# Seven column tiles of a projection as 2x2 block products with seven products (Strassen's form)

## The reference, cut to what matters

```python
xn = _rmsnorm(x, g_pre)          # x: 2048 prompt tokens and 8*8 sample tokens, 1024 wide
u = xn @ w_in                    # 1024 x IN_WIDTH, the part that the change touches
gq, gk, gv, gg, glr, dq, dk, dv, dg, ga, gb = jnp.split(u, cuts, axis=-1)
...
o_a, s_new = _gla(q, k, v, log_a, gla_s0)
...
o_g, lse_g = _dilated_prompt(qg, kg, vg, dil, span)      # g in three groups: (128,1), (512,4), (2048,16)
...
merged = jax.nn.sigmoid(ga) * y_a + jax.nn.sigmoid(gb) * y_b
h = x + _rmsnorm(merged @ w_out, g_post)
h = h + (pe @ w_ple_proj) * jax.nn.sigmoid(h @ w_ple_gate)
```

## Time and profile before

| | |
|---|---|
| time, median of 3 runs | 2802.56 us (2802.45 to 2804.43) |
| span of the profiled execution | 2799.7 us, 40580 instructions |
| time of the profiled execution itself | not recorded apart; its span is 2.9 us under the median |
| PE busy | 2769.4 us, 99% |
| DVE, ACT, POOL busy | 1077.3, 861.5, 360.3 us |
| column tiles 0 to 19 | about 0 to 2154 us |
| column tiles 9 to 15 | about 956 to 1723 us |
| the mix | about 2154 to 2800 us |

### The profile page before, as it was taken

One profiled execution on the slowest core, in us unless ns is written; L12 is line 12 of the kernel. 1 busy time (PEld: TensorE's weight loads), 2 busy tenths in 40 slices (PEclk: granted clock), 3 DMA queues, 4 the chain that ended last, 5 costly groups with the idle time before them and its releaser, 6 DMA issues.

```text
span 2799.7 us, 40580 instructions
## 1 busy us (share of the span) xinstructions
PE 2769.4 (99%) x16108; PEld 1453.6 (52%) x16108; DVE 1077.3 (38%) x2401; ACT 861.5 (31%) x1728; POOL 360.3 (13%) x601
## 2 busy tenths in 40 slices
PE   8999999999999999999999999999999899999998
PEld 4444456555545665666555555555544344444444
DVE  6211134444333443344223333333322655555452
ACT  5111124444312222333123321111112544444441
POOL 2000011111311002120011113222100000000000
PEclk9999999999999999999999999999999999999999
DMA  9543464655577566584576789787646966556642
GB/s 283 134 168 132 147 208 152 214 177 207 190 253 286 187 195 213 185 273 152 179 278 208 257 234 301 239 249 252 216 152 224 277 172 174 148 149 180 164 112 58
DMA packets 326542, 558.35 MB, mean 199 GB/s; under 512 B 179114, under 2 KB 184305, under 8 KB 321874
## 3 DMA queue, kind: packets, MB, share of 16 engines
q1 hardware_dynamic: 268722, 290.57, 34.9%
q0 software_dynamic: 43376, 231.63, 25.3%
q10 hardware_dynamic: 14256, 33.56, 3.3%
HBM read 378.70 MB, written 236.79 MB: 220 GB/s over the span
## 4 chain that ended last, share of the span: by engine, by line
PE 96%; DMA 1%; SPq 1%; DVE 1%; ACT 0%; issue 0%; POOL 0%; DVEq 0%; POOLq 0%
PE out L2654 40%; PE out L2214 22%; PE out L2651 18%; PE out L1143 2%; PE out L1128 2%; PE out L2657 2%; PE out L1134 1%; PE out L615 1%; PE out L626 1%; PE out L625 1%; PE out L1429 1%; PE out L1389 1%; DMA mix_pe_in<-in_p_prompt 1%; SPq L356 1%; PE out L1117 1%; PE out L1402 0%
## 5 line engine op out<-in xcount | busy, mean ns | idle before, releaser
L2654 PE MATMUL out<-w_hi,xn_hi 128*128 128x512 f16 x1792 | 679.9, 379 | 1.0 <-DVE w_lo L2514 0.5
L2654 PE MATMUL out<-w_lo,xn_hi 128*128 128x512 f16 x1792 | 679.4, 379 | 0.0
L2654 PE MATMUL out<-w_hi,xn_lo 128*128 128x512 f16 x1792 | 679.4, 379 | 0.0
L2545 ACT ACTIVATE stage<-out 128x512 f32<-128x512 f32 (+1 forms) x170 | 99.4, 585 | 926.9 <-PE out L2654 613.2
L2592 DVE TENSOR_SCALAR stage<-out 128x512 f32<-128x512 f32 (+1 forms) x170 | 114.7, 675 | 645.0 <-PE out L2654 398.4
L2651 PE MATMUL out<-xn_hi,w_hi 128*128 128x512 f16 x768 | 291.3, 379 | 0.0
L2651 PE MATMUL out<-xn_hi,w_lo 128*128 128x512 f16 x768 | 291.1, 379 | 0.0
L2651 PE MATMUL out<-xn_lo,w_hi 128*128 128x512 f16 x768 | 291.1, 379 | 0.0
L2654 PEld LDWEIGHTS out<-w_hi,xn_lo 128*128 128x128 f16 x1792 | 175.4, 98 | 211.5 <-issue 0.3
L2654 PEld LDWEIGHTS out<-w_hi,xn_hi 128*128 128x128 f16 x1792 | 175.8, 98 | 192.6 <-issue 6.2
L2654 PEld LDWEIGHTS out<-w_lo,xn_hi 128*128 128x128 f16 x1792 | 175.4, 98 | 186.4 <-issue 0.3
(11 more groups left out here) (320 smaller groups left out, 3950.5 us busy)
## 6 DMA issues: line engine op xcount, KB each, us to landing
out<-in_cache_kv_w POOLq DMA_DIRECT2D x64, 1020.0 KB, 9.8
U<-stage SPq DMA_DIRECT2D x224, 256.0 KB, 4.6
raw<-in_w_in SPq DMA_DIRECT2D x78, 512.0 KB, 5.1
UT<-stage SPq DMA_DIRECT2D x96, 256.0 KB, 4.2
sw_kc<-in_cache_kv_w ACTq DMA_DIRECT2D x24, 1024.0 KB, 9.6
sw_vc<-in_cache_kv_w POOLq DMA_DIRECT2D x24, 1024.0 KB, 9.4
sw_rows<-U POOLq DMA_DIRECT2D x32, 512.0 KB, 7.8
out<-in_cache_kv_w POOLq DMA_DIRECT2D x16, 1008.0 KB, 8.0
```

Of the source, the lines that this page charges most:

```text
L2545: move_out(act, m, lambda o, x: act.activation(o, x, ACT.Copy, scale=1.0 / W_SCALE))
L2654: last = pe.matmul(out[m % 3][:, :], x[:, k, at:at + P], y[:, k, :], start=first, stop=final)
```

## The change

Column tiles 9 to 15 are made in another way. The left factor of a pair of token tiles (256 tokens, 1024 deep) and a column tile of w (1024 deep, 512 wide) are both seen as 2x2 blocks. Seven products of sums of blocks (Strassen's form with Winograd's sums) stand in place of eight. A product is 4 slices times 3: 12 matmuls with 128x128 weights that move 256 columns (L703). A column tile is 8 pairs times 7 products and the sample tile between pairs 3 and 4: 57 units, spread over the same 34 slots (one or two in each: `unit_slot`).

- **Left sums** (class `Sums`): four sums of blocks of xn for each pair, made once by DVE in slots 58 to 129, split into hi and lo (ACT, DVE), and kept in DRAM (`X`). For each pair of each of the seven tiles SP loads two DMAs of 512 KB of them (L861) over the place of xn's odd tiles (`xn[part][:, 1, 4r:4r+4, :HALF_K]`, r = pair % 2). What stood there is kept in `KEPT` and comes back for tile 16 (L893).
- **Right sums**: SP loads the column tile whole (`w_block`, 2 MB). DVE makes four sums (slots 14, 16, 18, and after the first cut), and ACT and DVE cut seven operands into a ring of eight (`cut_hi` L754, `cut_lo` L758), the first at the end of pair 6 and the other six in pair 7 of the tile before. The ring lies where `w_hi`, `w_lo` were, and the sums where `raw` was.
- **Eviction**: products use three banks; products 3 to 6 add to what stands there. ACT copies 2 of 7 (256 wide), and DVE adds 5 of 7 to what is in `stage` (256 wide, L798).
- **Layout**: xn is now [part][odd/even][pair][slice][token], so that a moving operand of four token tiles (`four_tiles`, in the TURNED tiles and the low rank product) consists of four pieces of 128.
- **Order**: `ORDER` puts the last of the TURNED tiles ahead of tile 9, the windows start at slots 277, 385, 449 (before: 277, 351, 452) and the samples at 524 (527). k and v of the windows have one buffer and four parts in place of two buffers. Plain tile 16 starts with pieces 0 and 1 of its weights cut at the last product but one of tile 15, and pieces 2 and 3 in slot 0 of tile 16.

```diff
+SEVEN_FIRST, SEVEN_LAST = 9, 15
...
+    SUM = {1: 1, 2: 0, 4: 2, 5: 3}
+    SCALAR = {0: 1, 3: 2}
+    VECTOR = {1: 1, 2: 2, 4: 3, 5: 4, 6: 5}
...
+    def tensor(self, pe, n, slot, staged):
+        j = n - SEVEN_FIRST
+        for unit in units_at(slot):
...
+            pair, i = pair_of(unit)
+            bank = self.product_bank(j, pair, i)
+            self.wait_bank(pe, j, pair, i, staged)
+            if pair == 0:
+                pe.wait_ge(self.op_lo, j * PRODUCTS + i + 1)
+            if i == 1:
+                pe.wait_ge(self.sums_loaded[pair % 2], 32 * ((j * PAIRS + pair) // 2 + 1))
+            for k in range(HALF_K):
+                for order, (x, y) in enumerate(((0, 0), (0, 1), (1, 0))):
+                    last = pe.matmul(bank[:, :HALF], self.left(j, pair, i, x, k), self.right(j, i, y)[:, k, :],
+                                     start=i < 3 and k == 0 and order == 0, stop=k == HALF_K - 1 and order == 2, skip_group_check=True)
+            last.then_inc(self.made, 1)
...
+    def vector(self, dve, n, slot):
...
+                dve.scalar_tensor_tensor(out=part, in0=bank[:, :HALF], scalar=1.0 / W_SCALE, in1=lower[:, :HALF] if i < 3 else part,
+                                         op0=ALU.mult, op1=ALU.add).then_inc(self.vector_kept, 1)
+            if j + 1 < SEVENS:
+                if (pair, i) == (PAIRS - 2, 6):
+                    self.cut_lo(dve, j + 1, 0)
+                if (pair, i) == (PAIRS - 1, 0):
+                    self.add_blocks(dve, j + 1, 3)
+                if pair == PAIRS - 1 and i > 0:
+                    self.cut_lo(dve, j + 1, i)
...
+            if i == 5:
+                x = j * PAIRS + pair + 2
+                sp.wait_ge(self.made, self.made_at(j, unit))
+                if x < SEVENS * PAIRS:
+                    self.load_sums(sp, *divmod(x, PAIRS))
...
+                if n == SEVEN_LAST + 1 and q % TILE_SLOTS in (0, 1):
+                    for i in range(RAW):
+                        load_raw(sp, piece_of(n, RAW * (1 + q % TILE_SLOTS) + i))
```

More of the change, by code:

```diff
@@ L190, with seven, sample_place, plain_tiles @@
 CUT_SLOT, CUT_PERIOD = 170, 10
+SEVEN_FIRST, SEVEN_LAST = 9, 15
+SEVENS = SEVEN_LAST - SEVEN_FIRST + 1
+HALF_K = K_TILES // 2
+HALF = BANK // 2
+PAIRS = SEQ // (2 * P)
+PRODUCTS = 7
+UNITS = PAIRS * PRODUCTS + 1
+SAMPLE_UNIT = PAIRS // 2 * PRODUCTS
+W_RING, W_SHIFT = 8, 4
+SUM_SLOT, SUM_PERIOD = 58, 9
+def seven(n):
+    return SEVEN_FIRST <= n <= SEVEN_LAST
+def sample_place(n):
+    return PAIRS if seven(n) else TOKEN_TILES - 1
+def plain_tiles(n):
+    return sum(not seven(i) for i in range(n))
+def plain_before(m):
+    n, place = divmod(m, TOKEN_TILES)
+    return sum((i * TOKEN_TILES + t) % 2 == m % 2 for i in range(n + 1) if not seven(i) for t in range(TOKEN_TILES)
+               if i < n or t < place)
+def plain_made(m):
+    return plain_before(m) + 1
+def pair_of(unit):
+    return divmod(unit if unit < SAMPLE_UNIT else unit - 1, PRODUCTS)
+def unit_slot(unit):
+    return unit * TILE_SLOTS // UNITS
+def units_at(slot):
+    return [u for u in range(UNITS) if unit_slot(u) == slot]
+def pair_place(pair):
+    return 2 * pair if pair < PAIRS // 2 else 2 * pair + 1
 def wait(eng, sem, n):
@@ L416, in landed @@
     def landed(self, e, s, tiles):
-        return 16 * sum(2 if m % TOKEN_TILES == TOKEN_TILES - 1 else 1 for m in range(tiles) if m % 2 == e and m // 2 % 2 == s)
+        return 16 * sum(2 if m % TOKEN_TILES == sample_place(m // TOKEN_TILES) else 1 for m in range(tiles) if m % 2 == e and m // 2 % 2 == s)
     def wait_tiles(self, eng, tiles):
@@ L2303, in later, with later_load @@
             return Later(signal, base)
+        def later_load(name):
+            signal, base = next(left_loads, None) or (sem(name, start=0), 0)
+            return Later(signal, base)
         with ExitStack() as region:
-            samples = Samples((core.bind(region)[0], sem, later), side, U, caches, a["sample_mask"], identity, OG)
+            top = core.bind(region)[0]
+            top("sw_low", [P, (SIDE_BYTES - BLOCK_BYTES) // 4])
+            late = top("sw_new_k", [P, WIDTH]), top("sw_new_v", [P, WIDTH]), \
+                [top(f"sw_rows{s}", [P, Samples.PAIR, WIDTH]) for s in range(Samples.RING)]
+        with ExitStack() as region:
+            samples = Samples((core.bind(region)[0], later, later_load), late, side, U, caches, a["sample_mask"], identity, OG)
         with ExitStack() as region:
@@ L2364, in side_queue @@
                 q.wait_ge(empty_stored, 16)
+                sums.done(q)
             if slot == GLA_SLOT - 3:
```

785 lines of the change are left out of this document (620 added, 165 removed).

## The result

The changed kernel takes 2856.36 us (median, 2851.98 to 2860.96) where the kernel before takes 2802.51: slower, ratio 1.019 with a 95% interval of 1.0177 to 1.0202. The forecast was 2768 us with a range up to 2795. The profiled execution has a span of 2859.1 us, 59.4 more than before.

A forecast was written before the change was run, and what follows sets the result against it. PE's work was taken to bound the kernel. From 2802.56 us, -66.0 (matmuls) + 5 (four pieces) + 8 (DVE) + 2 (chains) + 7 (tile 15 to 16) + 10 (DMAs) = -34 gave 2768 us, range 2742 to 2795.

The forecast's parts named there:

- the DMAs: In tiles 9 to 15, 112 added loads make transfers short in tiles 14 and 15: 10 us, bounds 0 and 40.
- a sign of being wrong: The prediction is wrong if PE waits for `xn<-X` or for samples' loads by more than 25 us.
- a term of 4 us by that figure: The DMA cost in tiles 14 and 15 if the limit is about 358 GB/s: 4 us in place of 10.
- Matmuls, the gain: In seven tiles, 4704 matmuls of 256 columns at 109.3 ns replace 2688 at 215.8 ns: a gain of 66.0 us.
- rival 3: In the seven tiles' matmuls the weight load binds, 24 ns a matmul for handing over: +79 us, 2882 us, chance 0.06.
- The moving operand in four pieces: In six plain TURNED tiles, 2304 matmuls read four pieces of 128: 5 us, between 0 and 6.9.
- DVE at the ends of tiles: In the last five slots of tiles 9 to 14, PE waits for DVE's evictions, cuts and steps: 8 us.
- Waits for product 4 in each pair: A sign that the prediction is wrong: PE waits in each pair for the eviction of product 4.
- the 2 us for chains: In slots with one product, chains miss the 0.4 us margin between DVE's step and PE's next: 2 us.
- From tile 15 to 16: At the start of tile 16 PE waits 2.1 us, then 4.2 us, for weight cuts: 7 us, bounds 5 and 12.
- Rival 2: The bound moves to queues, DMA term 25 us and DVE's 15: -14 us, 2788 us, chance 0.19.
- Rival 1: Cover holds; DVE's lead, the DMAs and the joints cost 10 us in place of 32: 2748 us, chance 0.22.

The follow-up runs named there:

- e17: The kernel before, with 112 transfers of 512 KB added in tiles 9 to 15 that nobody reads: 2835.0 us, ratio 1.0112.
- e1: The changed kernel with the left sums loaded only twice in all, four loads in place of 112: 2767.0 us, ratio 0.987 to the kernel before.
- its two variants: The kernel before with cache copies moved out of tiles 9 to 15 (2803.5 us), and with 112 transfers of 512 KB added there (2835.0 us).
- the best version: The changed kernel with cache copies in tiles 1 to 8, kept rows later, tile 16's w pieces loaded ahead and w's block in eight loads: 2774.1 us.

## Why the prediction failed

**The step that failed is the DMAs.** It took 10 us with a bound of 40, "nearer to none, since PE was busy 109.00 of 109.00 us at 0.87". The runs put it at 89 us, clock included, and PE waits 57.1 us for `xn_lo<-X` where the prediction had named 25 us as a sign of being wrong. Three parts of it were wrong.
- The bound was made from means over the tiles 14 and 15 alone. PE is idle 44.6 us in these two, near the 44 us of shortage that was worked out for them. Another 47.3 us lie in tiles 9 to 13, for which the term had nothing. There the waits began, in tile 9, at a mean share of 0.83. What delays a load is the 15 to 30 us in which the engines are full (0.96 to 1.04), and a tile's mean hides them.
- A load of sums was to take "two times 5.1 us at worst" and to be issued 16 us ahead. The median landing is 9.2 us, within that, but the nine that PE waited for took 14.5 to 30.6 us. The lead was 11.2 us where no steps of the windows stand between the products, as in the wait shown (19.1 us to landing).
- That PE had borne 0.87 was evidence for the kernel before only. The run with as much traffic added (e17) shows that it bears 0.86 for seven tiles with a quarter of the idle time. The changed kernel does not. What is left as the difference is that PE waits for the new loads themselves, its shorter slots, its three banks and the stage stores on the same queue, but no run took these apart.

**A term that was missing is the clock.** No step had it. The waits drop the granted clock; 21.3 us of the 90 are this.

**The rate.** The prediction took 315 GB/s for full engines. Over the time from issue to landing of each of the nine loads they moved 270 to 362 GB/s, and 378 and 382 in the two rows at 1190 and 1199. The Trainium skill, "DMA: Bandwidth & Descriptors", section "Specifications", states about 358 GB/s as a core's limit to HBM. The rows at 1190 and 1199 stand above it, so it is not the ceiling here, and a term of 4 us by that figure would have been further off than the 10.

**Matmuls, the gain: the spacing was right.** Twelve in 1.31 us are 109 ns each. The weight load stayed at 98 ns and does not bind, so rival 3 is out. The section "Back-to-back issue gap" of "TensorE: Matmul & The Clock Gate" of the Trainium skill states 131 ns at 512 columns and 81 ns at 128. The traces show 215.8 ns and 57 ns, and now 109 ns at 256. The gain did not arrive as time: tiles 9 to 15 came out 61 us longer and not 50 shorter, with a DMA share of 14 and 15 at 0.88 and 0.93.

**The moving operand in four pieces: 0, not 5.** L3279 takes 379 ns as before.

**DVE at the ends of tiles: 2 to 3 us, not 8.** Both in the changed kernel and in that without sums PE waits 1.1 us for an eviction at the end of tile 10, where none was forecast, and 1.6 us for masks at the ends of tiles 12 to 14; an eviction measured 0.423. Waits for product 4 in each pair didn't come, nor did the 2 us for chains.

**From tile 15 to 16: 12 us, not 7.** The first wait is 3.3 us where 2.1 was worked out. The second is 8.8 us where it was 4.2, since the loads of `raw` there take up to 12.4 us to land and not 5.1. The sum is at the edge of the bounds.

**The rivals.** Rival 2 named the mechanism (loads of sums and stage stores share the engines while banks are free for one product) and had 25 us for it, where 89 were due. Slower had a chance of 0.06, all of it for the weight load (rival 3). Rival 1 said 10 us of costs and added 12. Without the loads of the sums the kernel takes 2767 us (e1), the forecast's own number: the forecast would have come true only if its 112 loads had cost nothing, and even then by luck, since it had 10 us for them and e1 has other waits in their place.

**Not forecast and not settled:** in the mix PE waits 8.6 us for `mix_zTl` in the kernel before, 6.9 and 9.0 in its two variants, and in no changed kernel. The reason was not tested. So some 9 us of the best version's 28 may come from elsewhere than the seven products.
